# A hybrid encoder block on eight cores: attention re-tiled to 8 rows by 16 columns, keys in 8x8 cells

## The reference, cut to what matters

```python
h = rms_norm(x, norm_g);  proj = h @ w_in                 # (L, 6144)
u, g_pool, q, k, v, g_na = split(proj)                    # 1024 columns each
pool_out = pool_mixer(u) * silu(g_pool)                   # centred means over 2/4/8/16 tokens, minus u, then w_pool
# attention: tokens form a grid of 64 columns; a query at (r, c) sees 8 rows, clip(r-4, 0, rows-8) onwards,
# and 16 columns, clip(c-8, 0, 48) onwards, with a relative bias rpb[head, dr, dc], and the 16 meta keys
p = softmax([q.km*0.125 + meta_bias, q.k*0.125 + rpb])    # 16 + 128 keys
na_out = (p_m @ vm + p_g @ v) * silu(g_na)
y = rms_norm(x + concat(pool_out, na_out) @ w_out, final_g)
```

## Time and profile before

| | us |
|---|---|
| median of 3 runs | 2065.19 |
| the profiled execution: its span | 2068.8 |
| projection stage, until TensorE starts on queries | 620.5 |
| attention stage | 618 |
| wait for loads between the stages, output stage | 830 |
| TensorE busy / VectorE / ScalarE / GpSimd | 1917.6 / 1216.8 / 937.4 / 186.3 |

### The profile page before, as it was taken

The page is one execution under the profiler, slowest core; times in us unless marked ns, Lnnn a source line. Parts: engine busy times, 40 slices in busy tenths (PEclk is TensorE's granted clock), DMA queues, the critical chain, the costliest instruction groups (busy, mean ns, idle before and its releaser), DMA issues. The chain is left out here.

```text
span 2068.8 us, 47325 instructions; the slowest of 8 cores (2051.9 to 2068.8 us)
## 1 busy us (share of the span) xinstructions
PE 1917.6 (93%) x16144; PEld 1017.5 (49%) x16144; DVE 1216.8 (59%) x2518; ACT 937.4 (45%) x1763; POOL 186.3 (9%) x299
## 2 busy tenths in 40 slices
PE   4899999999979869999999986999999999999998
PEld 1344444444445546566565663444444444444445
DVE  2244453333325758888888984556655566655564
ACT  2144432222216759999998981222232222222222
POOL 1212121112110100000000000000000000000000
PEclk9899999999999989999999987999999999999999
DMA  9856774435337994433433309632344322344212
GB/s 173 180 173 187 224 166 145 159 124 165 101 125 172 156 144 133 110 111 109 123 107 118 96 31 271 215 104 91 103 148 148 132 83 93 137 148 148 88 49 74
DMA packets 165815, 277.38 MB, mean 134 GB/s; under 512 B 61294, under 2 KB 93678, under 8 KB 160462
## 3 DMA queue, kind: packets, MB, share of 16 engines
q1 hardware_dynamic: 115806, 163.81, 27.1%
q0 software_dynamic: 49776, 110.54, 19.9%
HBM read 198.81 MB, written 101.40 MB: 145 GB/s over the span
## 5 line engine op out<-in xcount | busy, mean ns | idle before, releaser
L594 ACT ACTIVATE sb_PT<-bankpair 128x512 bf16<-128x512 f32 (+1 forms) x1000 | 508.0, 617 | 75.8 <-PE bankpair L587 70.0
L334 PE MATMUL bankpair<-sb_Wvu,sb_HT 128*128 128x512 bf16 x1632 | 367.5, 384 | 12.6 <-DMA sb_Wvu<-w_in 12.6
L846 PE MATMUL bankpair<-sb_Wo,sb_MIX 128*128 128x512 bf16 x1600 | 347.4, 379 | 2.8 <-DVE sb_PLT L778 1.9
L611 DVE TENSOR_TENSOR sb_PT<-sb_PT,sb_EB 128x512 bf16<-128x512 bf16 x632 | 249.0, 421 | 39.6 <-ACT sb_PT L594 25.6
L334 PEld LDWEIGHTS bankpair<-sb_Wvu,sb_HT 128*128 128x128 bf16 x1632 | 158.9, 99 | 199.9 <-issue 22.4
L846 PEld LDWEIGHTS bankpair<-sb_Wo,sb_MIX 128*128 128x128 bf16 x1600 | 155.6, 98 | 189.9 <-issue 4.1
L587 PE MATMUL bankpair<-sb_QT,sb_KR 64*128 64x128 bf16 x3200 | 180.9, 225 | 37.2 <-DVE sb_rec L640 24.7
L624 PEld LDWEIGHTS bankpair<-sb_VR,sb_PT 128*128 128x128 bf16 x3200 | 171.0, 100 | 62.1 <-issue 12.2
L852 ACT ACTIVATE sb_junk<-sb_Y 128x1024 bf16<-128x1024 f32 x50 | 52.9, 1057 | 315.6 <-DVE sb_Y L849 315.6
L314 PE MATMUL bankpair<-sb_HT,sb_Wk 128*128 128x512 bf16 (+2 forms) x896 | 182.2, 364 | 10.1 <-DMA sb_Wk<-w_in 4.5
L624 PE MATMUL bankpair<-sb_VR,sb_PT 128*128 128x65 bf16 x3200 | 185.2, 197 | 3.1 <-issue 2.5
(11 more groups left out here) (93 smaller groups left out, 2322.8 us busy)
## 6 DMA issues: line engine op xcount, KB each, us to landing
sb_X<-xall SPq DMA_DIRECT2D x51, 512.0 KB, 5.1
sb_XR<-xall SPq DMA_DIRECT2D x50, 512.0 KB, 7.4
y<-sb_O POOLq DMA_DIRECT2D x50, 512.0 KB, 3.7
sb_UW<-u_s SPq DMA_DIRECT2D x61, 256.0 KB, 4.1
v_s<-sb_Vs POOLq DMA_DIRECT2D x51, 260.0 KB, 2.8
kT_s<-sb_KTs POOLq DMA_DIRECT2D x51, 256.0 KB, 5.6
u_s<-sb_Us POOLq DMA_DIRECT2D x51, 256.0 KB, 2.7
sb_VR<-v_s SPq DMA_DIRECT2D x50, 260.0 KB, 5.1
```

The lines of the kernel that those rows point to most:

```text
L334: S.op('tensor', lambda e, pb=pb, cg=cg, kc=kc, hs=hs, j=j: e.matmul(banks[pb][:, :], HT[hs][:, kc, j * 128:(j + 1) * 128], Wvu[:, kc, cg ...
L594: S.op('scalar', lambda e, nk=nk, b=b, par=par, ps=ps, bk=bl[par]: e.activation(out=PT[ps][0:nk, b, par, :], in_=banks[bk][0:nk, :], func= ...
L611: S.op('vector', lambda e, ein=ein, pin=pin: e.tensor_tensor(out=pin(), in0=pin(), in1=ein(), op=ALU.mult), reads=[('PT', ps, b, par)], wr ...
L846: S.op('tensor', lambda e, po=po, kc=kc, cg=cg, j=j: e.matmul(banks[po][:, :], MIX[:, kc, j * 128:(j + 1) * 128], Wo[:, kc, cg * 512:(cg + ...
```

## The change

**Tokens.** A core now has 48 own tiles (12 chunks of 4) and a last chunk of three: 2 halo tiles and the meta tile. The halo tiles get K and V only: no U, no hidden states in DRAM, no queries, no output. Their V is written once before and once behind the own tokens, multiplied by a 0/1 flag per core. The output stage has 12 chunks instead of 13.

**Layout of keys.** K of a chunk (8 rows) is stored as eight cells of 8 rows by 8 columns, in one DMA; V is read from DRAM by cells, 64 rows of 2080 bytes.

**Attention tiles.** 14 tiles: ten of 8 grid rows, four of 4 rows at the borders. A tile is cut in 4 column groups of 16 (s), so that a unit is 128 (or 64) queries and 8 heads. There are 112 units. Groups s=1 and 2 need two pairs of cells from each of two chunks (4 blocks of 128 keys), s=0 and 3 one pair from each and a "combo" of one cell from each (3 blocks). A tile of 8 rows has 28 blocks. Of the border tiles two see one chunk only (16 blocks), two see two (28 blocks, of half the columns).

**Meta keys.** For each tile and G four matmuls with a stationary operand of 32 columns make the scores of 4 times 2 heads by 16 meta keys on 128 partitions, one `exp` with the bias added; their product with V is one matmul of 260 columns per unit and half, with a block-diagonal operand.

**Exponentials.** One `exp` and one table multiplication over both banks of a block (1024 columns).

**Tables** are prepared on the host as biases (with -30000 for masked places) and exponentiated in 44 pieces of 1024 columns, four behind each of chunks 1 to 11, through two staging buffers; 24 pieces go back to DRAM, as tables of the border tiles.

```diff
-                        evac(ev1(), lambda fc=fc, hs=hs, N=N: KTs[hs][:, fc, 0:N], lambda pb=pb, N=N: banks[pb][:, 0:N],
-                             [PS(pb)], [('KTs', hs)])
-                    for j in range(nt):
-                        t = t0 + j
-                        S.op('gpsimd', lambda e, hs=hs, t=t, j=j: e.dma_start(out=kT_v(t), in_=KTs[hs][:, :, j * 128:(j + 1) * 128]),
-                             reads=[('KTs', hs)], writes=[('kT_d', t)], dma=('sK', hs))
+                        kdst = lambda r0, nr, fc=fc, hs=hs: KTs[hs][:, fc, :].rearrange('p (e r c) -> p r e c', e=8, r=8)[:, r0:r0 + nr]
+                        ksrc = lambda nr, pb=pb: banks[pb][:, 0:nr * 64].rearrange('p (r e c) -> p r e c', r=nr, e=8)
+                        if ci < NCH:
+                            evac(ev1(), lambda kdst=kdst: kdst(0, 8), lambda ksrc=ksrc: ksrc(8), [PS(pb)], [('KTs', hs)])
+                        else:
+                            evac('scalar', lambda kdst=kdst: kdst(0, 4), lambda ksrc=ksrc: ksrc(4), [PS(pb)], [('KTs', hs)])
+                            evac('scalar', lambda kdst=kdst: kdst(4, 4), lambda ksrc=ksrc: ksrc(4), [PS(pb)], [('KTs', hs)])
+                            evac('scalar', lambda fc=fc: KMs[:, fc, :], lambda pb=pb: banks[pb][:, 256:384], [PS(pb)], ['KMs'])
+                    S.op('gpsimd', lambda e, hs=hs, ci=ci: e.dma_start(out=kT_d[ci], in_=KTs[hs][:]),
+                         reads=[('KTs', hs)], writes=[('kT_d', ci)], dma=('sK', hs))
+                    if ci == NCH:
+                        S.op('gpsimd', lambda e: e.dma_start(out=km_d, in_=KMs[:]), reads=['KMs'], writes=['km_d'], dma='sKM')
...
-                    for cg in range(4):
+                    cgs = [0, 1, 2, 3] if (main or j == 2) else [0, 1]
+                    us = None
+                    for cg in cgs:
...
+                STG = [sb(es, 'STG%d' % i, [128, 1024], F32) for i in range(2)]
+                STB = [sb(es, 'STB%d' % i, [128, 1024], BF16) for i in range(2)]
+                pieces = [('f', i, q) for i in range(4) for q in range(4)] + [('c', i, q) for i in range(2) for q in range(2)]
+                pieces += [('x', i, q) for i in range(4) for q in range(6)]
...
+                def p1_table(pi):
+                    kind, i, q = pieces[pi]
+                    sg = pi % 2
+                    sl = slice(q * 1024, (q + 1) * 1024)
+                    if kind == 'x':
...
+                    S.op('sync', lambda e, src=src: e.dma_start(out=STG[sg][:], in_=src()),
+                         writes=[('STG', sg)], dma=('STG', sg))
+                    S.op('scalar', lambda e, dst=dst: e.activation(out=dst(), in_=STG[sg][:], func=AF.Exp),
+                         reads=[('STG', sg)], writes=[res])
+                    if kind == 'x':
+                        S.op('gpsimd', lambda e: e.dma_start(out=xtab_d[i][:, sl], in_=STB[sg][:]),
+                             reads=[('STB', sg)], writes=[('xtab', i, q)], dma=('sST', sg))
...
-                    if 1 <= ci <= 4:
-                        p1_tables(ci - 1)
+                    if ci >= 1:
+                        for _ in range(4):
+                            if tpi < len(pieces):
+                                p1_table(tpi); tpi += 1
...
+                TILES = [dict(t0=0, nq=4, ch=[0], xs=0, special=0)]
+                TILES += [dict(t0=(8 * i + 4) * 64, nq=8, ch=[i, i + 1], xs=None) for i in range(3)]
+                TILES += [dict(t0=28 * 64, nq=4, ch=[3], xs=1, special=0)]
+                TILES += [dict(t0=2048, nq=4, ch=[4, 5], xs=2, special=1)]
+                TILES += [dict(t0=2048 + (8 * i + 4) * 64, nq=8, ch=[i + 5, i + 6], xs=None) for i in range(7)]
+                TILES += [dict(t0=2048 + 60 * 64, nq=4, ch=[12, 13], xs=3, special=0)]
+                NTL = len(TILES)
+
+                qplace = lambda c: (c, 0 if c == 0 else 1) if c < 4 else (c + 1, 0 if c == 4 else 1)
+                FILL = {0: 1, 1: 2, 2: 3, 4: 4, 5: 5}
+                FILL.update({t: t for t in range(6, 12)})
...
+                def qbank():
+                    b = st2['qb']; st2['qb'] = 13 - b
+                    return b
...
+                def p2_qmm(ci, fc, kc):
+                    if kc == 0:
+                        qstate[(ci, fc)] = qbank()
                     pb = qstate[(ci, fc)]
...
+                    if kc == KC - 1:
+                        ta, pa = qplace(ci)
+                        for hh, (t, pl) in enumerate(((ta, pa), (ta + 1, 0))):
+                            evac('scalar' if fc % 4 == 0 else 'vector',
+                                 lambda t=t, pl=pl: QT[t % 3][:, fc, :, pl * 64:pl * 64 + 64].rearrange('p s (r c) -> p s r c', r=4),
+                                 lambda hh=hh: banks[pb][:, hh * 256:hh * 256 + 256].rearrange('p (r s c) -> p s r c', r=4, s=4),
+                                 [PS(pb)], [('QT', t % 3)])
+
+                def p2_meta(t, G):
+                    n = TILES[t]['nq'] * 16
+                    pb = qbank()
+                    for jj in range(4):
+                        S.op('tensor', lambda e, jj=jj, fc=4 * G + jj: e.matmul(
+                            banks[pb][32 * jj:32 * jj + 32, 0:4 * n], KM[:, fc, :], QT[t % 3][:, fc, :, 0:n],
+                            start=True, stop=True),
+                             reads=KMR + [('QT', t % 3)], writes=[PS(pb)])
+                    S.op('scalar', lambda e: e.activation(
+                        out=PM[t % 2][:, G, :, 0:n], in_=banks[pb][:, 0:4 * n].rearrange('p (s q) -> p s q', s=4), func=AF.Exp,
+                        bias=mbP[:, G:G + 1], scale=0.125),
+                         reads=[PS(pb), 'mbP'], writes=[('PM', t % 2, G)])
...
+                    for k, i in enumerate(tl['ch']):
+                        pairs = {0: [0], 1: [0, 1], 2: [1, 2], 3: [2]}[s]
+                        for o, q in enumerate(pairs):
...
+                    if s in (0, 3):
+                        w = s // 3
+                        nk = 64 * len(tl['ch'])
+                        b = dict(nk=nk, parts=[(i, 7 * w, 1, 64 * k) for k, i in enumerate(tl['ch'])], V=VC[w],
+                                 vres=[('VC', w, k) for k in range(len(tl['ch']))])
...
+                        for (i, cell, ncell, p0) in bl['parts']:
+                            for par in range(2):
+                                S.op('tensor', lambda e, jj=jj, fc=fc, i=i, cell=cell, ncell=ncell, p0=p0, par=par: e.matmul(
+                                    banks[2 * sp + par][p0:p0 + 64 * ncell, jj * n:(jj + 1) * n],
+                                    KR[i % 3][par * 64:(par + 1) * 64, fc, cell:cell + ncell, :].rearrange('p e n -> p (e n)'),
+                                    QT[t % 3][par * 64:(par + 1) * 64, fc, s, 0:n],
+                                    start=True, stop=True),
+                                     reads=[('KR', i % 3), ('QT', t % 3)], writes=[PS(2 * sp + par)])
+                    S.op('scalar', lambda e: e.activation(
+                        out=PT[ps][0:nk, bi, :, 0:n].rearrange('p (a b) q -> p a b q', a=2),
+                        in_=bank2[sp][0:nk, :].rearrange('p (a m) -> p a m', a=2)[:, :, 0:4 * n].rearrange('p a (b q) -> p a b q', b=4),
+                        func=AF.Exp, scale=0.125),
+                         reads=[PS(2 * sp), PS(2 * sp + 1)], writes=[('PT', ps, bi)])
+                    hs = slice(G * 8, G * 8 + 8)
+                    S.op('vector', lambda e: e.tensor_tensor(
+                        out=PT[ps][0:nk, bi, :, 0:n], in0=PT[ps][0:nk, bi, :, 0:n], in1=bl['E'](hs), op=ALU.mult),
+                         reads=[('PT', ps, bi), bl['eres']], writes=[('PT', ps, bi)])
...
+                    S.op('tensor', lambda e: e.matmul(
+                        banks[4 + par][0:n, 0:260], PM[t % 2][:, G, s, 0:n], VMb[:, G, par, :, :].rearrange('p a b -> p (a b)'),
+                        start=True, stop=False), reads=[('PM', t % 2, G)] + VMR, writes=[PS(4 + par)])
...
+                def pv_steps(ui):
+                    nb = len(unit_blocks(units[ui]))
+                    steps = [[], [], []]
+                    steps[0].append(lambda: p2_pvmeta(ui, 0))
+                    for bi in range(nb - 1):
+                        steps[0].append(lambda bi=bi: p2_pv(ui, 0, bi, False))
+                    steps[1].append(lambda: p2_pv(ui, 0, nb - 1, True))
+                    steps[1].append(lambda: p2_norm(ui, 0))
+                    steps[1].append(lambda: p2_pvmeta(ui, 1))
+                    for bi in range(nb):
+                        steps[1 if bi < 2 else 2].append(lambda bi=bi: p2_pv(ui, 1, bi, bi == nb - 1))
+                    steps[2].append(lambda: p2_norm(ui, 1))
+                    return steps
...
+                    if s == 0 and G == 0:
+                        c = FILL.get(t)
+                        fill = [(c, fc, kc) for fc in range(KC) for kc in range(KC)] if c else []
```

(34 more changed lines are left out.)

711 lines of the change are left out of this document (333 added, 378 removed).

## The result

The changed kernel takes 2089.8 us (median) against 2065.2; the ratio of the two is 1.0116, 95% interval [1.0083, 1.0149], taken without one run of 2346.7 us in which four cores had a granted clock of 0.80. It is slower, where faster was forecast. The profiled execution of after is the quickest of its runs, 2081.4 us with a span of 2079.9: set against the 2068.8 of the earlier trace rows the trace shows 11.1 us of the 24 by which the medians differ. The rest lies between executions and no trace here shows where.

The account below looks back on a forecast made before the run. TensorE was taken to bound the projection stage, ScalarE the attention stage with TensorE close behind. From the span, 2068.8 - 34 - 12.8 + 69 - 43 = 2048.0, less 3.6 gives 2044 us; 8-in-10 range 1985 to 2090.

Parts of the forecast that it names:

- Part 1: Output stage: one chunk of two tiles goes and nothing takes its place, a gain of 34 us.
- Part 2: Projection stage, work that falls away: U of two halo tiles 6.9 us, the fourth table round's loss 5.9; together -12.8.
- The 5.9 of the fourth round: Projection stage: the old fourth table round made its chunk take 49.1 us instead of 43.2; its small tables go, -5.9.
- Part 3: Projection stage: late staging loads hold ScalarE's queue, 6.4 us per round, +69 us in all, between 36 and 110.
- T+1.6: Projection stage: T starts the key groups behind a round; 1.6 us later the first exponential ends, allowing the third load.
- Rival (c): Projection stage: border pieces wait for stores, input tiles land late; a round costs 10 us, +41, total 2085; chance 0.18.
- part 4: Attention stage: TensorE becomes the bound, a full tile takes 43.5 us, the stage 575 for 618: -43, between -85 and 0.
- rival (b): Attention stage: bank clash covered and no half clock, 38.7 us per full tile, 38 less, total 2006; chance 0.13.
- bank clash: Attention tile: both meta groups take one bank, so query group 1 gets group 0's and waits 1.4 us (0 to 2).
- the 3.4 us for half clock: Attention tile: each of two waits brings a 3.4 us stretch at half clock, 1.7 us lost each.
- same bytes in fewer microseconds: Attention stage's congested start: conversions move the same bytes in less time; a loss of 20 us of today's 35 (5 to 40).
- the 1.0 and 0.6 in the sum: Attention tile, TensorE: meta scores taken as 1.0 us, four combo groups of 16 instructions instead of 8 as 0.6.

Follow-up runs that it names:

- h3: Kernel before, each of its four table rounds loaded in two halves through one buffer of half the size, second load late: 2115.0 us, ratio 1.0252.
- h5: Changed kernel with three staging and four bf16 buffers instead of two and two: 2028.0 us, ratio to before 0.9826.
- e2: Changed kernel with four staging buffers instead of two, still two bf16 buffers: 2043.3 us, ratio to before 0.9873.
- e3: Changed kernel with four bf16 buffers instead of two, still two staging buffers: ratio to before 1.0130.
- e1: Changed kernel with four staging and four bf16 buffers, so all loads of a round go out a round ahead: 1997.3 us, ratio to before 0.9662.
- h2: Changed kernel with each round of four pieces cut into two rounds of two, no buffer added: 1986.5 us, ratio to before 0.9623.
- e4: Changed kernel with the input tiles asked for ahead of a round's staging loads: 2079.7 us, ratio to before 1.0060.
- g3: On top of e1, the twelve weight conversions spread from units 4 to 15 to every fifth unit up to 59: ratio to before 0.9550.

## Why the prediction was wrong

**Part 1** (output, -34): right, 34.4, and nothing took its place.

**Part 2** (-12.8): right. From the twelfth store of hidden states to the first query matmul before has 620.5 - 579.8 = 40.7 us, the kernel with rounds of two pieces 616.4 - 582.2 = 34.2: 6.5 for a forecast of 6.9. The 5.9 of the fourth round are gone too. The first chunk's store comes 4.3 us later than before on core 5, but that is no effect of the change: over the eight cores it comes at 99.3 to 103.5 us before and at 97.5 to 105.0 after, 101.2 in the mean of both.

**Part 3** is the step that failed, in size and not in mechanism. Ten rounds cost 99.3 us and the last about 8 (42.2 us behind it for 34.2): 107 for a forecast of 69, and the whole sign hangs on these 38 us. The chain was the one forecast: third load issued at T+1.6 (200.17), no spare buffer, square, table load, root, bank. Of the 35 us by which ten rounds missed their 64, the waits are 29 (74.0 for 45, 7.4 a round for 4.5) and what they bring behind them 6 (25.3 for 19). Three terms were too small. First, the fourth piece: forecast at T+8.6, two microseconds behind the third; it came at T+11.7, some 9 us after its issue. That is the median of the earlier trace rows, which I had set aside because "the queue is otherwise quiet just then"; it was not, as the full DMA row from 205 us shows. So this piece, and not the input tile forecast last at T+11, held ScalarE's queue: the tile's square follows it without a wait. In the round shown, the mildest of the ten, the bank was free at T+16.0 for a forecast of T+14.9, the wait 5.64 for 4.5; the mean of the five main rounds is 6.3. Second, what a wait brings behind it: 1.9 was taken from the wait of 4.03 in the earlier trace rows; over the ten rounds it was 2.5 in the mean, between 1.7 (behind 10.06) and 3.1 (behind 7.68), behind 10.59 (h3) 2.9, behind 3.53 (h5) 1.5. Third, border rounds: their waits are 8.4 us in the mean, and they cost 11.1 each instead of 6.4; e2 and e3 show that the late store alone brings 8.8 of it and the late loads alone 10.0.

e1 and h2 show it from one side (rounds with early loads are free), h3 from the other (the old kernel with late ones loses 14 us a round), h5 in between. Why the fourth load takes 9 us is shown only so far: the DMA engines are full, and it is not the input tiles (e4). The Trainium skill (ScalarE: Activation LUTs, What ACT_TABLE_LOAD costs) has a drain beside each table load; in e1 the exponential starts at 187.76, 0.02 behind the end of the load begun at 186.46, so this trace doesn't agree, and h2 with ten more pairs of switches is no slower than e1, so leaving the drain out of the sum was right.

**Rival (c)** is the case that came in: 10 us a round, and it decided at the point named, above 8.7. That its 2085 lies so near the 2089.8 is in part luck: as a span it is 2089 for the 2079.9 of the trace, since it left part 4 as it stood, which came out 12 us better. Of the 38 us that rival (b) saw there, the six full tiles behind the start gave 18. Its reasons were half right. The store is a wait of its own (e2), but not on top of the loads (e3); and the input tiles, its other half, carry 1 to 2 us (e4). With the landing times of the earlier trace rows at 4.5 to 12.5, median 9.2, a forecast that took 5 for each of eleven rounds should have given this rival more than 0.18.

**Part 4** (-43, measured -54.7): right in its bound and its work, with two errors that partly cancel. The work: 1025 ns for a two-bank exponential (forecast 0.98), 0.69 for the product of 1024 columns (0.65). Waits of a full tile: QT 15.0 us in 8, bank clash 9.2 in 7, 1.9 and 1.3 each (2.2 and 1.4 forecast), seen in the waits from 857 us on:

```profile
PE bankpair L621 <- DVE sb_QT L187: 15.0, 8, 2.2
PE bankpair L640 <- DVE sb_ATT L667: 9.5, 25, 1.0
PE bankpair L550 <- ACT sb_QT L189: 9.2, 7, 1.6
```

But full tiles took 38.7 to 41.7, not 43.5. Of four of them with the same two waits, 1.94 us for QT and 1.34 at the bank clash, two ran at a clock of 0.96 and took 41.2, two at 1.00 and took 39.9 and 40.2. One of each kind, cut at the stores of a tile's last part:

```profile
987.85:1027.74 39.89, 36.24 (x572) 21.96 (x568) 30.51 (x72) 30.21 (x35) 2.42 (x5) 1.00 0.52 170
1109.14:1150.35 41.21, 37.64 (x571) 22.47 (x568) 30.42 (x72) 30.34 (x35) 2.39 (x5) 0.96 0.37 111
```

At full clock TensorE is busy for 36.2 us, where the sum said 36.5. The error was the 3.4 us for half clock, 1.7 for each wait. In the tile between 1109 and 1150 TensorE waits for QT until 1141.07 and at the bank clash until 1148.49 (the stretches around them):

```profile
1140.80:1144.20 3.40, 3.13 (x32) 1.74 (x32) 1.55 (x5) 1.60 (x2) 0.00 (x0) 0.61 0.97 398
1144.20:1147.60 3.40, 2.96 (x44) 1.32 (x40) 1.21 (x3) 2.42 (x3) 0.00 (x0) 0.89 0.57 234
1147.60:1151.00 3.40, 2.51 (x35) 1.62 (x36) 1.75 (x4) 1.92 (x5) 0.60 (x1) 1.00 0.16 42
```

The longer wait is followed by clocks of 0.61 and 0.89, (0.39 + 0.11) x 3.4 = 1.7 us lost, the shorter by none. That alone takes half of the 3.4 away, and the tiles at a clock of 1.00 have not even this. By the sum, 36.5 + 1.9 + 1.3 = 39.7 without and 41.4 with it. What decides which tile is hit, no run here shows. The six full tiles behind the start take 242.9 us, 18 less than forecast. The start took 11 more: the first three tiles 165.8 us, where 17.2 of queries, 31 and two full tiles of 43.5 and a loss of 20 were put (155.2); taken against tiles of 41.2 the loss is 35, as large as before's. The part "same bytes in fewer microseconds" was seen and undersized, and it is less the bytes than the queue: the stores of finished tiles stand behind the conversions, VectorE waits 28.8 us for them in four waits between 720 and 857, and g3 has no such wait in its first 143 us. Tiles without queries took 33.0 and 31.7 (31), border tiles 29.1, 39.2 and 22.9 (31, 40, 23).

The second place where the Trainium skill was weighed (TensorEngine Tiling (Array Packing), Key Properties: matmuls on different tiles of the array run in parallel) went its way: four meta matmuls of 256 columns on four column tiles take 0.29 us (of 512 columns, as a full tile has them, 0.40, and a full tile has two such groups), and a combo group of 16 takes 0.42 where 8 take 0.40. So the 1.0 and 0.6 in the sum should have been at most 0.8 and nothing.

```profile
739.38 0.29 PE L566 MATMUL bankpair<-sb_QT,sb_KM 128*32 128x256 bf16 x4
```

```profile
1110.71 0.42 PE L621 MATMUL bankpair<-sb_QT,sb_KR 64*64 64x128 bf16 x16
...
1111.94 0.40 PE L621 MATMUL bankpair<-sb_QT,sb_KR 64*128 64x128 bf16 x8
```

## What to carry to other kernels

When a change makes a burst of work longer than its ring of buffers, look at when the loads past the ring can be issued: the second half of the burst costs a full landing time in an in-order queue, in every repetition, and the cure may be to cut the burst rather than to buy buffers (2090 to 1986 us here). A wait that the trace names can have a twin beside it that ends as late; only taking away both, or each in turn, tells. For a term that counts eleven times, take the median of the landing times that the trace shows, not the hopeful end, and list what else is issued in the same microseconds. A transfer that nobody waits for can still hold a store that somebody does, if both stand in one queue.

## What the runs showed of the hardware

Single waits of TensorE of 3.5 to 10.6 us in the projection stage cost 1.5 to 3.1 us more than their length: the granted clock is 0.50 and 0.73 in the two stretches of 3.4 us behind the one of 5.64. The surcharge doesn't grow with the wait: 3.1 behind 7.68, 1.7 behind 10.06. In the attention stage a wait of 1.94 us drew 1.7 us of half clock in two tiles (clock 0.96) and none in two others that are alike in all that the trace shows of TensorE's waits (clock 1.00), so a price per short wait is a mean at best. Of two loads of 0.5 MB issued some 1.1 us apart, with a store of 1 MB beside them and four input tiles behind them, the first landed after 5.4 us and the second after 8.8, with the DMA engines full at 432 GB/s. And stores of 0.25 MB behind conversions in GpSimd's queue landed after 22.9 us (e1), where with few of them ahead they took 4.9 (g3).
